# Thirty-two by thirty-two block turns on VectorE, and a DRAM round trip, in place of TensorE transposes for the memory attention

## What is computed

```python
x = x + mixed @ w_out[l]
mem_n = rms_norm(mem, norm_mem_src[l])
x = x + memory_cross_attention(rms_norm(x, norm_mem_x[l]), mem_n, w_mem_q[l], w_mem_kv[l], w_mem_o[l])
x = x + hierarchical_moe(rms_norm(x, norm_ffn[l]), ...)
```

## Time and profile before

| | us |
|---|---|
| three runs | 1357.63, 1356.27, 1355.04 (median 1356.27) |
| the profiled execution | 1355.84 |
| its span, first to last instruction | 1354.1 |
| TensorE busy (share of the span) | 998.5 (74%) |
| VectorE busy | 579.0 (43%) |
| ScalarE busy | 300.4 (22%) |
| moved by DMA | 486.40 MB, mean 359 GB/s |

### The profile page before, as it was taken

One profiled execution on the slowest core, in us unless ns is written; L12 is line 12 of the kernel. 1 busy time (PEld: TensorE's weight loads), 2 busy tenths in 40 slices (PEclk: granted clock), 3 DMA queues, 4 the chain that ended last, 5 costly groups with the idle time before them and its releaser, 6 DMA issues.

```text
span 1354.1 us, 20680 instructions
## 1 busy us (share of the span) xinstructions
PE 998.5 (74%) x8540; PEld 600.2 (44%) x8540; DVE 579.0 (43%) x1114; ACT 300.4 (22%) x521; POOL 52.4 (4%) x108
## 2 busy tenths in 40 slices
PE   8999999999999985666655566655566654566656
PEld 7888898888888532222212222222222221222222
DVE  5555566886657543223332233332223332223324
ACT  5554457674455100000000000000000000000002
POOL 1300001231000000000000000000000000000001
PEclk9999999999999998778787787787777877777878
DMA  7778763448869999999999999999999999999997
GB/s 247 263 238 255 217 167 123 144 136 273 286 252 338 358 417 428 433 430 432 433 430 434 432 432 434 433 429 433 429 434 432 433 433 433 430 432 430 433 426 303
DMA packets 78020, 486.40 MB, mean 359 GB/s; under 512 B 9943, under 2 KB 25437, under 8 KB 64798
## 3 DMA queue, kind: packets, MB, share of 16 engines
q1 hardware_dynamic: 77484, 483.46, 88.7%
q10 hardware_dynamic: 306, 2.11, 0.4%
q0 software_dynamic: 192, 0.31, 0.2%
HBM read 481.14 MB, written 4.72 MB: 359 GB/s over the span
## 4 chain that ended last, share of the span: by engine, by line
PE 51%; DMA 46%; SPq 1%; DVE 1%; issue 1%; ACT 0%; DVEq 0%; ACTq 0%
DMA gu<-in_w_up 42%; PE ps L1052 10%; PE ps L605 8%; PE ps L607 8%; PE ps L606 8%; PE ps L1107 5%; DMA down<-in_w_down 4%; PE ps L1031 2%; PE ps L1064 1%; PE ps L585 1%; PE ps L850 1%; PE ps L851 1%; PE ps L852 1%; PE ps L778 1%; SPq L470 0%
## 5 line engine op out<-in xcount | busy, mean ns | idle before, releaser
L1052 PE MATMUL ps<-gu,xe 128*32 128x256 f32 x3968 | 286.3, 452 | 306.0 <-DMA gu<-in_w_up 305.5
L2138 DVE TENSOR_TENSOR x_sum<-ps,x_sum 128x512 f32<-128x512 f32 x240 | 149.1, 684 | 507.6 <-PE ps L1064 507.6
L1052 PEld LDWEIGHTS ps<-gu,xe 128*32 128x32 f32 x3968 | 140.5, 129 | 469.3 <-DMA gu<-in_w_up 328.7
L1616 DVE TENSOR_TENSOR w_lo<-w_raw,w_hi 128x1024 fp32r<-128x1024 f32 (+1 forms) x137 | 164.6, 1208 | 118.1 <-ACT w_hi L1225 114.8
L605 PE MATMUL ps<-w_hi,a_hi 128*128 128x512 f32 (+1 forms) x468 | 183.4, 392 | 0.0
L606 PE MATMUL ps<-w_lo,a_hi 128*128 128x512 f32 (+1 forms) x468 | 179.7, 384 | 0.0
L607 PE MATMUL ps<-w_hi,a_lo 128*128 128x512 f32 (+1 forms) x460 | 176.8, 384 | 0.0
L1225 ACT ACTIVATE w_hi<-w_raw 128x1024 fp32r<-128x1024 f32 (+1 forms) x137 | 141.8, 1039 | 127.1 <-PE ps L607 88.6
L1535 ACT ACTIVATE sg<-ps 128x128 f32<-128x128 f32 x31 | 8.6, 278 | 654.3 <-PE ps L1052 654.3
L1107 PE MATMUL ps<-down,act_t 128*32 128x512 f32 x976 | 112.8, 603 | 5.3 <-DMA down<-in_w_down 5.3
L606 PEld LDWEIGHTS ps<-w_lo,a_hi 128*128 128x128 f32 x468 | 88.0, 188 | 16.4
(11 more groups left out here) (341 smaller groups left out, 854.9 us busy)
## 6 DMA issues: line engine op xcount, KB each, us to landing
down<-in_w_down SPq DMA_DIRECT2D x29, 4096.0 KB, 22.7
gu<-in_w_gate SPq DMA_DIRECT2D x28, 4096.0 KB, 31.7
gu<-in_w_up SPq DMA_DIRECT2D x28, 4096.0 KB, 41.0
w_raw<-in_w_in SPq DMA_DIRECT2D x56, 512.0 KB, 4.9
w_raw<-in_w_out SPq DMA_DIRECT2D x32, 512.0 KB, 4.7
gu<-in_w_up SPq DMA_DIRECT2D x18, 512.0 KB, 6.6
w_raw<-in_w_mem_kv SPq DMA_DIRECT2D x16, 512.0 KB, 3.5
down<-in_w_down SPq DMA_DIRECT2D x13, 512.0 KB, 15.5
```

Source lines behind the costliest of these rows:

```text
L1052: mm = pe.matmul(ps[5][j * SLOTS:(j + 1) * SLOTS, 0:2 * P].rearrange("s (m f) -> s m f", m=2), xe[:, k, :], gu[side][:, :, k, j * P:(j + 1 ...
L1616: ve.tensor_tensor(w_lo[:, u % RING, :, 0:n], w_raw[:, u % RING, :, 0:n], w_hi[:, u % RING, :, 0:n], ALU.subtract).then_inc(S("w_split"), 1)
L2138: ins = ve.tensor_tensor(x_sum[:, t, cols], ps[g][:, :], (x_res if first else x_sum)[:, t, cols], ALU.add)
```

## The change

The memory is loaded by SP as eight pieces of 32 tokens, laid out so that partition block q holds columns 512q to 512q+511 (2 KB a partition). ScalarE sums the squares of each piece (eight of 512 columns in place of two of 2048), VectorE transposes each piece in place in 32x32 blocks, and the hi and lo parts are made from SBUF. The sums of squares, now spread over four partition blocks, are brought together by a GpSimd product with a folded identity and two small matmuls against a column of ones. The contracted dimension comes out in another order, so the rows of w_mem_kv and the gain are loaded in that order: a unit of these is two DMAs of 256 KB in place of one. For three quarters of the residual the same is done through the DRAM scratch: three more entries in QUADS, with x_res as the source and nat[:, 0] as the landing place, two in-place transposes of 128x512 on VectorE for each (memx_turn), hi and lo parts from SBUF, and three quarters of w_mem_q and of its gain in the new row order. The last quarter keeps its TensorE transposes. Counts of semaphores that shift by one are left out below.

```diff
+MEM_AT = [START[SB_Q] + 6 + _j for _j in range(SEQ // QUAD)]
...
-QUADS = [SB_Q, SB_Q + 1, SB_K, SB_K + 1, MEM_K]
+QUADS = [SB_Q, SB_Q + 1, SB_K, SB_K + 1, MEM_K, W_OUT + 1, W_OUT + 3, W_OUT + 5]
 MOVE_AT = [DONE[_c] + RING + 3 for _c in QUADS]
+X_MOVED = QUADS.index(W_OUT + 1)
+X_QUADS = len(QUADS) - X_MOVED
...
-        SPLIT_BANK.append(6 + _b % 2 if _name == "mem" else 4 + _b % 4)
+        SPLIT_BANK.append(None if _name == "mem" or _name == "memx" and _i < UK * X_QUADS else 4 + _b % 4)
...
-        mem_junk = place("mem_junk", [P, D], offset=km_at)
-        mem_sb = place("mem_sb", [P, TT, D], offset=o_at)
+        mem_junk = place("mem_junk", [P, UN], offset=km_at)
+        mem_spread = place("mem_spread", [P, TT * NJ, QUAD], offset=km_at + 2048)
+        quad_eye = place("quad_eye", [P, QUAD], offset=km_at + 3072)
+        mem_quads = place("mem_quads", [P, TT * NJ, UN], offset=o_at)
+        mem_turned = mem_quads[:, :, :].rearrange("p j (k s) -> p k j s", k=KD)
...
-            if QUADS[n] == MEM_K:
-                return nat[:, 1].rearrange("p t (j f) -> p (t j) f", f=P)
+            if QUADS[n] >= MEM_K:
+                return nat[:, 1 if n < X_MOVED else 0].rearrange("p t (j f) -> p (t j) f", f=P)
             return quads[:, n % 2]
 
         first_turns = [ps[4][:, 0:SEQ], ps[2][:, 0:SEQ]]
+
+        def by_quads(c, i):
+
+            return MEM_K <= c <= MEM_V or c == MEM_Q and i < UK * X_QUADS
...
-                return [cols(w_mem_kv, (c - MEM_K) * UN)]
+                return [w_mem_kv[0, :, (c - MEM_K) * UN:(c - MEM_K + 1) * UN].rearrange(
+                    "(q k r) n -> k q r n", q=NJ, r=QUAD)[i * UK:(i + 1) * UK]]
...
+            if c == MEM_Q and by_quads(c, i):
+                q, b = divmod(i, UK)
+                return [w_mem_q[0, q * UN:(q + 1) * UN, :].rearrange(
+                    "(q k r) n -> k q r n", q=NJ, r=QUAD)[b * UK:(b + 1) * UK]]
...
+                    if gain is norm_mem_src:
+                        src = gain[0].rearrange("(q k r) -> k q r", q=NJ, r=QUAD)
+                    else:
+                        src = gain[0].rearrange("(k p) -> k p", p=P)
+                    sp.dma_start(g_nat[r0:r0 + rows, :], src).then_inc(S("gains_loaded"), 16)
+                for q in range(NJ):
+                    rows = norm_mem_x[0, q * UN:(q + 1) * UN]
+                    sp.dma_start(g_nat[32 + 4 * q:36 + 4 * q, :], rows.rearrange("(k p) -> k p", p=P) if q >= X_QUADS
+                                 else rows.rearrange("(q k r) -> k q r", q=NJ, r=QUAD)).then_inc(
+                                     S("gains_loaded"), 16)
...
+                src = nat[:, NAT[c]] if n < X_MOVED else x_res[:, :, (n - X_MOVED) * UN:(n - X_MOVED + 1) * UN]
+                sp.dma_start(spill[n].rearrange("(t p) f -> p t f", p=P), src).then_inc(
                     S("spilled"), 16)
                 sp.wait_ge(S("spilled"), 16 * (n + 1))
                 if c == MEM_K:
                     sp.wait_ge(S("turned"), bank0[MEM_Q])
+                elif n >= X_MOVED:
+                    sp.wait_ge(S("split_lo"), SPLIT0["memx"] + 4 * (n - X_MOVED))
...
+                if by_quads(c, i):
+                    for k in range(UK):
+                        sp.dma_start(dst[:, k, :], src[k]).then_inc(S(f"w_loaded{u % RING}"), 16)
...
+                if u in MEM_AT:
+                    j = MEM_AT.index(u)
+                    sp.dma_start(mem_quads[:, j, :], mem[0, j * QUAD:(j + 1) * QUAD, :].rearrange(
+                        "s (q f) -> q s f", q=NJ)).then_inc(S("mem_loaded"), 16)
...
-            pe.wait_ge(S("mem_loaded"), 16)
+            pe.wait_ge(S("mem_spread"), 1)
+            for t in range(TT):
+                mm = pe.matmul(ps[7][:, t:t + 1], mem_spread[:, NJ * t:NJ * (t + 1), :].rearrange(
+                    "p j s -> p (j s)"), ones[:, 0:1], start=True, stop=True)
+            mm.then_inc(S("squares_summed"), 1)
             for n, (c, i) in enumerate(LATENT):
                 hi, lo = (cq_hi, cq_lo) if c < K_NOPE else (ckv_hi, ckv_lo)
                 if c in STANDING:
                     project_standing(c, i, hi, lo)
                 else:
                     project_units(c, [i], 0, hi, lo)
-                if n < KD // 2:
-                    split_turn("mem", mem_sb, 2 * n, 2 * n + 2)
...
                 project(W_OUT + 2 * q)
-                pe.wait_ge(*chunk_out(W_OUT + 2 * q - 1))
-                if q == 1:
-                    pe.wait_ge(S("sums_made"), 1)
-                split_turn("memx", x_res, 4 * (q - 1), 4 * q)
                 project(W_OUT + 2 * q + 1, a0=HEADS)
...
+            def mem_squares(t):
+
+                for j in range(NJ):
+                    sc.wait_ge(S("mem_loaded"), 16 * TT * NJ)
+                    square(mem_quads[:, NJ * t + j, :], chunk_ss[:, t, j:j + 1], mem_junk[:, :])
+                    sq[0] += 1
+                    sc.wait_ge(S("squared"), sq[0])
...
+                if SB_K <= c < SB_V:
+                    mem_squares(c - SB_K)
...
+            def mem_heads(k):
+
+                if k == 0:
+                    sc.wait_ge(S("w_used"), START[Q_PE])
+                    sc.wait_ge(S("split_turned"), (SPLIT0["mem"] + KD) // 2)
+                sc.activation(a_hi[:, k, :].rearrange("p (j s) -> p j s", s=QUAD), mem_turned[:, k], ACT.Copy,
+                              scale=g_t[:, 16 + k:17 + k]).then_inc(S("split_hi"), 1)
...
-                split_head("memx", 32, hi=a2_hi, k_from=4 * q, k_to=4 * q + 4)
+                if q == X_QUADS:
+                    split_head("memx", 32, hi=a2_hi, k_from=4 * q, k_to=4 * q + 4)
+                else:
+                    for k in range(4 * q, 4 * q + 4):
+                        sc.wait_ge(S("split_turned"), (SPLIT0["memx"] + k) // 2 + 1)
+                        sc.activation(a2_hi[:, k, :].rearrange("p (j s) -> p j s", s=QUAD),
+                                      quads_of(X_MOVED + q)[:, :, k % 4 * QUAD:(k % 4 + 1) * QUAD], ACT.Copy,
+                                      scale=g_t[:, 32 + k:33 + k]).then_inc(S("split_hi"), 1)
...
+            def turn_mem(t):
+
+                ve.wait_ge(S("squared"), 3 * TT + NJ * (t + 1))
+                for j in range(NJ * t, NJ * (t + 1)):
+                    ve.transpose(mem_quads[:, j, :], mem_quads[:, j, :]).then_inc(S("split_turned"), 1)
+
             for c in range(Q_LAT, Q_PE):
                 split_w(DONE[c] + RING)
+                if c >= SB_V:
+                    turn_mem(c - SB_V)
...
+            def mem_rest(k):
+
+                ve.wait_ge(S("split_hi"), SPLIT0["mem"] + k + 1)
+                ve.scalar_tensor_tensor(
+                    out=a_lo[:, k, :].rearrange("p (j s) -> p j s", s=QUAD), in0=mem_turned[:, k],
+                    scalar=g_t[:, 16 + k:17 + k],
+                    in1=a_hi[:, k, :].rearrange("p (j s) -> p j s", s=QUAD), op0=ALU.mult,
+                    op1=ALU.subtract).then_inc(S("split_lo"), 1)
...
+            def memx_turn(q):
+
+                ve.wait_ge(S("quads_loaded"), 16 * NJ * (X_MOVED + q + 1))
+                for b in range(2):
+                    tile = quads_of(X_MOVED + q)[:, :, b * UK * QUAD:(b + 1) * UK * QUAD]
+                    ve.transpose(tile, tile).then_inc(S("split_turned"), 1)
...
                 split_w(DONE[c] + RING - (1 if c == W_OUT else 0))
+                if c > W_OUT and (c - W_OUT) % 2 == 0:
+                    memx_turn((c - W_OUT) // 2 - 1)
                 add_heads(c)
...
+            for q in range(1, NJ):
+                link(gp.tensor_tensor(quad_eye[:, :], ident[:, 0:QUAD] if q == 1 else quad_eye[:, :],
+                                      ident[:, q * QUAD:(q + 1) * QUAD], ALU.add))
+            gp.wait_ge(S("squared"), 3 * TT + TT * NJ)
+            gp.tensor_tensor(
+                mem_spread[:, :, :],
+                quad_eye[:, :].rearrange("p (a s) -> p a s", a=1).to_broadcast([P, TT * NJ, QUAD]),
+                chunk_ss[:, :, :].rearrange("p t j -> p (t j)").rearrange(
+                    "p (j a) -> p j a", a=1).to_broadcast([P, TT * NJ, QUAD]),
+                ALU.mult).then_inc(S("mem_spread"), 1)
+            norms([SS_MEM], D, "sums_made", 1)
```

More of the change, by code:

```diff
@@ L368, in load_small @@
             def load_small():
-                for gain, r0, rows in ((norm_mem_src, 16, 16), (norm_mem_x, 32, 16),
+                for gain, r0, rows in ((norm_mem_src, 16, 16),
                                        (norm_q_lat, 48, 4), (norm_kv_lat, 52, 2), (norm_mla_out, 54, 8),
                                        (norm_sb_out, 62, 8), (norm_ffn, 70, 16)):
-                    sp.dma_start(g_nat[r0:r0 + rows, :], gain[0].rearrange("(k p) -> k p", p=P)
-                                 ).then_inc(S("gains_loaded"), 16)
+                    if gain is norm_mem_src:
[8 more added lines that the diff above has]
+                                     S("gains_loaded"), 16)
                 for t in range(TT):
@@ L1751, in _ @@
                 if n < KD // 2:
```

(27 more changed lines are left out.)

29 lines of the change are left out of this document (11 added, 18 removed).

## The result

The changed kernel takes 1402.85 us (median of four runs, 1397.57 to 1405.5) against 1356.49 for the kernel before (four runs, 1355.04 to 1357.63): a ratio of 1.0338, 95% interval 1.0303 to 1.0372. It was forecast 4.4 us faster and is 46 us slower. The profiled execution took 1405.5 us, its span is 1403.8.

The account below looks back on a forecast made before the run. TensorE, never idle in most of the first half, was taken as the bound there: 6.4 us removed, 0.5 and 1.5 added, so 4.4 us less than 1356.27, forecast 1351.9 us, range 1349.4 to 1359.0.

Parts of the forecast that it names:

- I cost all this at nothing: Memory's added VectorE and ScalarE work and extra SP load issues, 0.37 us each: no cost, covered by four units of lead.
- Carried one to one: From TensorE's first half to the end: any shift of TensorE shows in full, since it hands back the buffers.
- The memory's 3.7 us: Memory stage: removing eight groups of four TensorE transposes, 0.46 us each, saves 3.7 us; two small matmuls add 0.5.
- The residual's 0.89 us a group: W_OUT stage: removing three groups of eight residual transposes from TensorE saves 0.89 us each, 2.7 us together.
- The stalls: W_OUT stage: TensorE waiting on the residual's three moves through DRAM, taken as 1.5 us, between nothing and 6.0.
- The first move: W_OUT stage, first residual quarter: unit ready at 336.5, wanted at 336.1; a stall of 0.4 us, or 1.2.
- Rival (a): Residual's moves: late read-backs stall TensorE, 12 us giving 1362; chance of slower 0.17, of no change 0.22.
- Rival (b): From 303 us on: the moves' extra 3.1 MB cost 9 us and the gain is lost, 1365; within the 0.17.

Follow-up runs that it names:

- e1: The changed kernel with every load gathered from four runs of rows cut by partition block, leading dimension 32; 1361.18 us, ratio 1.0042 to the kernel before.
- e11: e4 with the eight pieces of the memory behind every second unit's load in place of every one; 1355.01 us against 1355.81 for the kernel before.
- e10: e1 with only two residual quarters moved, turned one chunk later, the third left to TensorE; 1354.83 us against 1356.65 for the kernel before.
- e12: e10 with the memory's pieces spaced as in e11; 1354.23 us against 1355.81 for the kernel before.
- e4: e1 without the three moves of the residual, all four quarters transposed by TensorE; 1356.69 us, ratio 1.0004 to the kernel before.
- e5: The kernel before with the memory's key, value and query weights gathered from 2, 8 and 16 runs of rows; one execution, 1397.19 us.
- e8: e1 with the three moves of the residual issued on GpSimd's queue in place of SyncE's; 1380.58 us, ratio 1.0164 to the kernel before.

## Why the prediction was wrong

**The step that failed** is in the paragraph on the memory: "The memory's loads pass from one 2 MB transfer of ScalarE's queue to eight of SP's, and 22 units are loaded in two halves: more issues of 0.37 us each", and "I cost all this at nothing". I counted the issues and took their price from a row of loads whose leading dimension is 128. No row showed a load gathered from four runs, and I gave this term no bounds. An issue took 2.46 us of SP's program and not 0.37, the ordinary loads between were held too (up to 3.58 us), and the shape cost 41.7 us of time (the changed kernel less e1). The Trainium skill (DMA: Bandwidth & Descriptors, section Why a DMA increments its semaphore by 16 and not by 1) says it: the number of engines is the largest one up to 16 that divides the slowest dimension of both access patterns. The shares 0.14 and 0.27 for two and four runs agree (2/16 and 4/16 are 0.125 and 0.25). In the prediction I drew on this page of the Trainium skill for the spill alone.

**Carried one to one**: right for a delay. TensorE's first gather is 47.5 us late in the changed kernel (498.33 against 450.85), the time 46.4; in e1 it is 5.1 late, the time 5. For a gain it isn't shown: of e11's 2.1 us the time has about 1.

**The memory's 3.7 us**: the mechanism right, the size off. 2.6 us is the gain, and 0.4 is lost ahead of it, where the two small matmuls stand: 2.1 net at V_MLA in e11, where I had 3.2. The price of a group was read rightly, and the other seven read in the same way cost about as much, 0.44 us. Where I went wrong was to take the matmuls around them as unchanged. One group of the kernel before, and a place in e11:

```profile
198.38 0.28 PE L625 MATMUL ps<-cq_hi,w_lo 128*128 128x256 f32 x1
198.50 0.60 PE L585 MATMUL ps<-ident,mem_sb 128*128 128x128 f32 x4
...
199.06 0.28 PE L624 MATMUL ps<-ckv_lo,w_hi 128*128 128x256 f32 x1
```

```profile
199.72 0.28 PE L660 MATMUL ps<-ckv_hi,w_lo 128*128 128x256 f32 x1
200.15 0.39 PE L658 MATMUL ps<-ckv_hi,w_hi 128*128 128x256 f32 x1 [0.15 <-ACT q_t L1425]
```

Around the last six groups stand 144 matmuls that hold the weights. In the kernel before most of them start 0.113 us apart, in e11 all 0.118, which takes back 0.5 us (why is open). And TensorE, now earlier, loses 0.3 us at 199.72, where it waits for ScalarE's q_t. That the new loads were free was wrong here too: 0 to 3.7 us of waits before 175 us as long as the pieces stood behind every unit.

**The residual's 0.89 us a group**: right. The hi*hi matmuls behind the first and second group start 0.89 and 1.79 us earlier in e1 than in the kernel before, against their distance at 303 us. **The stalls**: 1.5 us taken, at most 6.0, about 8.1 measured in e1 (2.7 removed, 5.4 lost net between 305 us and the gather). Of these 3.9 stand at the second move and about 4.2 from 387 us on, at the queries' late loads, while my sum followed the read-backs alone. The first move was the one without spare by my sum, and cost nothing. For the second I had the quarter added at 340.9, the last read-back landed at 351.7, the unit ready at 358.0 and wanted at 358.8. It was 342.03, about 353.6, 359.64 and 357.61. The add came late because the split ahead of it (339.48) waited for ScalarE's rounding, and that for a weight that SP had held back in the first move; the spill landed in 7.0 us and not 6.6 (median of three, by source), and TensorE came 1.2 us earlier: I had taken off the 0.89 of the second group alone, and not that of the first or what the memory's part brings. Rival (a) names this mechanism, with 17% for slower. That its 1362 is near e1's 1361.2 is luck: it has 12 us of stalls against 5.9 gained, e1 8.1 against 3.0. And 1.7 us of the largest stall is the clock's, which none of my sums contained. Rival (b), the moves' bytes, found no support: e10 and e12 move two thirds of them, 6 of its 9 us, and are not slower than e4 and e11.

The rule of the Trainium skill (VectorE: DVE Perf Modes, section Rules for kernel authors) that 128x128 blocks are for TensorE did not decide: VectorE's turns of the memory in place took 0.668 us, and no wait of TensorE shown here is for them. What cost was bringing the data into the shape they need.

## What to carry to other kernels

When an edit rearranges a DMA, read the first dimension of both its sides before counting its issues: a rearranged layout that put a count of 4 there moved 103 GB/s, where the experts' loads move 433, and the issuing engine showed it as long issues. Bound every new form of transfer from both sides, also the one that looks like bookkeeping. And give a round trip through DRAM a stage of room before an in-order engine has to read it: read one chunk later, the first two moves made TensorE wait 0.3 us at the most, in place of 2.0. Look as well at what the issuing engine loads next, since that comes late by about the time that it stood still (9.6 us for the queries).

## What the runs showed of the hardware

- A queue that is held by narrow transfers holds the issuing engine: 2.46 us an issue with four runs, 5.0 with two, and up to 3.58 for full-width loads issued between narrow ones, against 0.37 alone.
- Eight and sixteen runs made the issue itself 0.60 us where the queue was not held, against 0.38 for tiles in one run (e5).
- Behind the wait of 2.0 us near 360 us in e1 TensorE's granted clock was 0.66 over 5 us, and the matmuls started 0.43 us apart in place of 0.23, so that it cost 3.9 us. In the changed kernel the clock was 0.70 over 30 us with 11.7 of them idle. Not every such wait was followed by it: behind 2.2 us in e8 (95.3 us) it was 1.00.
- Matmuls of 128x256 that hold the weights started 0.113 us apart behind groups of transposes, and 0.118 in one long row (e11); why is open.
- A read-back of 128 KB landed in 2.6 us from SP's queue and in 7.8 us from GpSimd's (e1, e8; twelve each, medians), amid the same weight loads.
